# Operand and linear-attention steps of blocks 1 to 3 go two to a slot instead of one

## The chip, the cores and the metric

One core of a Trainium2 chip runs the whole kernel. The metric is device time in microseconds (us), from launch to end. The engines are PE (TensorE: matmuls, which accumulate in PSUM), DVE (VectorE), ACT (ScalarE), POOL (GpSimd) and SP (SyncE, which here only issues DMAs). Each engine works through its own list of instructions in order and waits on semaphores that others raise.

## The reference

One decoder layer on a sequence of 2048 rows of width 1024. The input projection feeds three token mixers in parallel, an output projection joins them, and a gated feed-forward part follows.

```python
h = rms_norm(x, norm1_gain) * (1.0 + scale1) + shift1
proj = h @ w_in
out_a = rg_lru(conv(xa), ...) * gelu(ya)                 # recurrence over the sequence
out_b = forgetting_attention(fq, fk, fv, ff, ...)        # 6 heads of 64, causal, RMS-normed q and k
out_c = gated_linear_attention(gq, gk, gv, glow, gg, ...)# 4 heads of 64, chunks of 64 rows
x = x + gate1 * (concatenate([out_a, out_b, out_c]) @ w_out)
h = rms_norm(x, norm2_gain) * (1.0 + scale2) + shift2
gt, up = split(h @ ffn_w_gate_up)                        # 2 x 2816 columns
x = x + gate2 * ((silu(gt) * up) @ ffn_w_down)
```

## The kernel before

The sequence is cut into four blocks of 512 columns (block 0 to block 3), everything transposed. A first function projects blocks 0 to 2 and runs their recurrence. The function that the change touches, `mix_and_feed_forward`, does the rest: the projection of block 3, and for each block the operands of the softmax attention, the linear attention, the softmax attention, the output projection and the feed-forward part.

**Units and slots.** Its backbone is a list `units` of 328 weight tiles: `p` (projection of block 3), `o` (output projection), `g` and `u` (gate and up), `d` (down). A unit is 8 (for some `d` units 6) triples of matmuls of 512 columns, since every float32 product is split into three (`split_products`, L77 to L79). A slot is one unit's place in this order. For each unit SP loads the tile, ACT rounds it to a high part (L1108), POOL subtracts it to get the low part (L1093), and PE multiplies into one of two PSUM banks (`ff_acc_ps`). The bank is read by ACT for `g` (a silu, L1280) or by DVE for `u` (L1575) and `d`. PE may start unit j + 2 only when unit j has been read. In ACT's and DVE's lists the reading of unit j stands behind all side work of slot j.

**Side work.** The table `side` hangs other work on slots. One entry is a "turn": a list of steps that PE does together between two triples of that unit; several turns in a slot are spread over its triples. ACT and DVE do the same steps in the same order, after reading unit j - 1. The work for block b sits in the slots of the unit run ahead of block b's output projection:

- `X`, steps 0 to 6, operands of the softmax attention: transposes of the values (L1718), squares and row sums (step 1 and 2, L1726), forget-gate sums on DVE (step 2, L1433 to L1447), norms (step 3, L1450 to L1459), and in steps 4 to 6 the spreading of the norms over q and k (L1744), two tiles in each, whose results SP writes to DRAM (L956, L959).
- `G`, steps 0 to 7 for each of two head pairs j, in the order `G_ORDER`: (0,0) (1,0) (0,1) (1,1) (0,2) (1,2) (0,3) (1,3) (0,4) (0,5) (0,6) (1,4) (0,7) (1,5) (1,6) (1,7), as (pair, step). Step 0 to 3 make the decays; step 2, called the gating step below, is a chain of five DVE operations (L1486 to L1497) with four exponentials on ACT behind it (L1209 to L1212). Step 4 transposes and multiplies, step 5 makes the outer products (L1772), from which DVE builds the running state in 16 dependent operations (L1522); step 6 needs the state (L1781, L1784); step 7 normalises (L1789 on PE, L1228 and L1230 on ACT, L1529 and L1533 on DVE).
- the heads of the softmax attention, as turns of `S` (scores for the maximum, L1665), `M` (the maximum turned, L1675, after DVE's L1395), `T` (scores, L1691), `V` (times the values, L1707) and `F`. A turn mostly holds one `T` and one `V`, often an `S`. They fill the slots from the end of the linear attention to six slots ahead of the block's output projection, however many those are.

`x_load`, `g_load`, `a_load`, `fill_at` and `q_fill` name the slots in which SP loads the inputs of these three parts and POOL presets their tiles. In block 0, whose side work has only the 24 `p` slots, `X` and `G` already stand two to a slot (`G0_SLOT`; steps 0 and 1 of `G` even four), set by code that the change leaves alone.

Of the kernel before, what the change touches and what calls it, by code (L numbers as in the profile page):

```python
# [42 lines left out]
GLA_T = GLA_HEADS * HEAD_DIM // P  # L43
# [513 lines left out]
def mix_and_feed_forward(nc, vec, mod, held, xT, w_in, w_gates, w_alpha, w_out, w_gate_up, w_down, consts, fox_rows, proj, mix, q_split, ka, kb, v_split, yT):  # L557
# [90 lines left out]
    X_STEPS, G_STEPS, X_LEAD, G_LEAD, A_LEAD, END = 7, 8, 3, 3, 2, 6  # L648
# [7 lines left out]
    side = {}  # L656
# [12 lines left out]
    for b in range(1, NBLK):  # L669
        turns = turns_of(b)  # L670
        lo = at["o", 0, 0, 0] + 1 if b == 1 else at["o", b - 1, KD - 1, 0] + 1
        x_load.append(lo)
        lo += X_LEAD
        for s in range(X_STEPS):
            side[lo + s] = [[("X", (b, s))]]
        lo += X_STEPS + 1
        g_load.append(lo)
        lo += G_LEAD - 1
        for x, (j, s) in enumerate(G_ORDER):
            side[lo + x] = [[("G", (b, j, s))]]  # L680
        lo += GLA_T * G_STEPS + 1
        a_load.append(lo)
        fill_at.append(lo)
        q_fill.append(lo)
        lo += A_LEAD - 1
        hi = at["o", b, 0, 0] - END
        for x, turn in enumerate(turns):
            side.setdefault(lo + x * (hi - lo) // len(turns), []).append(turn)
# [1258 lines left out]
```

## Time and profile before

| | |
|---|---|
| median of 3 runs | 2987.01 us (2985.84 to 2988.37) |
| the profiled execution's own time | 2993.32 us |
| its span, first to last instruction | 2991.5 us |
| PE busy | 2818.5 us, 94% |
| DVE, ACT, POOL busy | 49%, 40%, 35% |
| mean granted clock of TensorE | 0.973 of 2.4 GHz |
| chain that ended last | PE 64%, of it L77 to L79 49%; DVE 7%, ACT 4% |

The profiled execution took 6.3 us more than the median, so a difference read in the trace is to be set against 2993.32 us and then carried over to the median. A matmul's end in the trace is modelled, so PE counts as busy while it only drains; the time of PE is better counted by how many matmuls start in a stretch. "Granted clock" 1.00 is 2.4 GHz and 0.5 is 1.2 GHz, and a value between them is a mean over time at either.

### The profile page before, as it was taken

The page shows a single profiled execution, that of the slowest core. Times are in us where ns is not written, and L with a number is a line of the kernel's source. Part 1 is how long each engine was busy: PE and PEld are TensorE (multiplying, and loading weights), DVE is VectorE, ACT ScalarE, POOL GpSimd, SP SyncE. Part 2 cuts the span into 40 slices and gives each one's busy share as a digit, 9 for nine tenths or more (in the row PEclk, how much of TensorE's full clock was granted, in tenths as well). Part 3 has the DMA queues.
Part 4 walks back from the last instruction along what each step waited for, and adds up shares of the span by engine and source line. Part 5 has one row for each costly group of instructions (what it writes and reads, how often), then busy time and mean ns, then how long its engine had stood idle before and what let it go on. Part 6 is the DMA issues. An engine that isn't in the chain of part 4 may idle for free.

```text
span 2991.5 us, 32965 instructions
## 1 busy us (share of the span) xinstructions
PE 2818.5 (94%) x12416; PEld 2211.5 (74%) x12416; DVE 1463.1 (49%) x1876; ACT 1185.2 (40%) x1654; POOL 1035.5 (35%) x488
## 2 busy tenths in 40 slices
PE   8998998788988999999999999999999999999999
PEld 4786876466757777886777777867777777778887
DVE  3968786466564334435443454463435554421111
ACT  3333333343345244444433545454335455332222
POOL 2545453221324332243333222334332112444443
PEclk9999999789999999999999999999999999999999
DMA  7555535525644344444624454545245553423233
GB/s 266 180 167 178 166 130 162 171 78 159 220 123 138 105 134 130 130 152 145 184 74 126 140 150 123 161 149 173 74 130 150 151 150 114 144 98 96 94 99 92
DMA packets 159902, 419.05 MB, mean 140 GB/s; under 512 B 18284, under 2 KB 20604, under 8 KB 156672
## 3 DMA queue, kind: packets, MB, share of 16 engines
q1 hardware_dynamic: 157408, 412.48, 44.6%
q10 hardware_dynamic: 2336, 4.46, 0.4%
q8 instruction: 99, 1.62, 0.2%
q14 instruction: 59, 0.48, 0.1%
HBM read 355.95 MB, written 60.92 MB: 139 GB/s over the span
## 4 chain that ended last, share of the span: by engine, by line
PE 64%; DVE 7%; ACT 4%; issue 3%; DMA 3%; SPq 2%; POOL 1%; ACTq 0%; POOLq 0%; DVEq 0%
PE ff_acc_ps L77 17%; PE ff_acc_ps L78 16%; PE ff_acc_ps L79 16%; DMA ff_w_raw<-in_w_gate_up 2%; PE fa_st_ps L1691 1%; PE fa_o_ps L1707 1%; PE fa_s_ps L1665 1%; PE fa_st_ps L1692 1%; PE fa_o_ps L1709 1%; PE fa_o_ps L1708 1%; PE fa_s_ps L1666 1%; DVE ff_silu L1371 1%; DVE fa_inv_sum L1408 1%; SPq L956 1%; PE fa_o_ps L1781 1%
## 5 line engine op out<-in xcount | busy, mean ns | idle before, releaser
L1093 POOL TENSOR_TENSOR w_lo<-ff_w_raw,w_hi 128x1024 fp32r<-128x1024 f32 (+1 forms) x326 | 771.9, 2368 | 1626.7 <-PE ff_acc_ps L79 1553.7
L77 PE MATMUL ff_acc_ps<-h_odd_hi,w_hi 128*128 128x512 f32 x1856 | 752.2, 405 | 50.7 <-DVE h_odd_lo L1376 13.4
L78 PE MATMUL ff_acc_ps<-h_odd_lo,w_hi 128*128 128x512 f32 x1856 | 738.3, 398 | 0.0
L79 PE MATMUL ff_acc_ps<-h_odd_hi,w_lo 128*128 128x512 f32 x1856 | 736.7, 397 | 0.0
L1108 ACT ACTIVATE w_hi<-ff_w_raw 128x1024 fp32r<-128x1024 f32 (+1 forms) x326 | 338.7, 1039 | 935.8 <-PE ff_acc_ps L79 721.5
L77 PEld LDWEIGHTS ff_acc_ps<-h_odd_hi,w_hi 128*128 128x128 f32 x1856 | 357.2, 192 | 160.2 <-issue 63.6
L79 PEld LDWEIGHTS ff_acc_ps<-h_odd_hi,w_lo 128*128 128x128 f32 x1856 | 356.7, 192 | 78.4
L78 PEld LDWEIGHTS ff_acc_ps<-h_odd_lo,w_hi 128*128 128x128 f32 x1856 | 358.2, 193 | 72.7 <-issue 1.7
L77 PE MATMUL ff_acc_ps<-ff_a_hi,w_hi 128*128 128x512 f32 x704 | 285.2, 405 | 10.1 <-issue 6.1
L1401 DVE TENSOR_TENSOR fa_p_lo<-fa_probs,fa_p_hi 128x512 fp32r<-128x512 f32 x240 | 154.4, 644 | 286.7 <-ACT fa_p_hi L1142 286.4
L78 PE MATMUL ff_acc_ps<-ff_a_lo,w_hi 128*128 128x512 f32 x704 | 280.2, 398 | 0.0
L79 PE MATMUL ff_acc_ps<-ff_a_hi,w_lo 128*128 128x512 f32 x704 | 279.9, 398 | 0.0
L211 POOL TENSOR_TENSOR w_lo<-w_raw,w_hi 128x1024 fp32r<-128x1024 f32 x74 | 183.1, 2475 | 219.4 <-PE g_ps L79 163.2
L1141 ACT ACTIVATE fa_probs<-fa_st_ps 128x512 f32<-128x512 f32 x240 | 128.3, 535 | 230.3 <-PE fa_st_ps L1692 151.7
L1383 DVE TENSOR_REDUCE fa_ch_max<-fa_s_ps 128x1 f32<-128x512 f32 (+1 forms) x240 | 144.6, 607 | 137.9 <-PE fa_s_ps L1666 80.5
L1575 DVE TENSOR_TENSOR ff_gated<-ff_silu,ff_acc_ps 128x512 f32<-128x512 f32 x88 | 60.4, 687 | 309.0 <-PE ff_acc_ps L79 272.2
L250 ACT ACTIVATE w_hi<-w_raw 128x1024 fp32r<-128x1024 f32 x74 | 78.4, 1059 | 281.2 <-DMA w_raw<-in_w_in 254.2
L1577 DVE TENSOR_TENSOR ff_a_lo<-ff_gated,ff_a_hi 128x512 fp32r<-128x512 f32 x88 | 110.2, 1252 | 121.3 <-ACT ff_a_hi L1287 121.3
L77 PEld LDWEIGHTS ff_acc_ps<-ff_a_hi,w_hi 128*128 128x128 f32 x704 | 133.1, 189 | 46.4 <-issue 14.8
L77 PE MATMUL g_ps<-h_even_hi,w_hi 128*128 128x512 f32 x384 | 158.0, 411 | 9.8 <-POOL w_lo L211 5.6
L79 PEld LDWEIGHTS ff_acc_ps<-ff_a_hi,w_lo 128*128 128x128 f32 x704 | 133.4, 189 | 32.3
L78 PEld LDWEIGHTS ff_acc_ps<-ff_a_lo,w_hi 128*128 128x128 f32 x704 | 133.3, 189 | 32.0 <-issue 1.7
(263 smaller groups left out, 4047.5 us busy)
## 6 DMA issues: line engine op xcount, KB each, us to landing
ff_w_raw<-in_w_gate_up SPq DMA_DIRECT2D x176, 512.0 KB, 4.1
w_raw<-in_w_in SPq DMA_DIRECT2D x74, 512.0 KB, 4.3
ff_w_raw<-in_w_down SPq DMA_DIRECT2D x64, 512.0 KB, 3.6
mod_w<-in_w_mod SPq DMA_DIRECT2D x24, 1024.0 KB, 5.5
fa_v<-v_split_dram SPq DMA_DIRECT2D x60, 384.0 KB
ff_w_raw<-in_w_out SPq DMA_DIRECT2D x32, 512.0 KB, 3.9
fa_ks_a<-ka_dram SPq DMA_DIRECT2D x60, 256.0 KB
fa_kt_a<-ka_dram SPq DMA_DIRECT2D x60, 256.0 KB
```

Source lines behind the costliest of these rows:

```text
L77: nc.tensor.matmul(out, hi, act_hi, start=first, stop=False)
L78: nc.tensor.matmul(out, hi, act_lo, start=False, stop=False)
L79: return nc.tensor.matmul(out, lo, act_hi, start=False, stop=last)
L211: nc.gpsimd.tensor_tensor(w_lo[:, j % LO], w_raw[:, j % RAW], w_hi[:, j % HI].bitcast(F32), ALU.subtract).then_inc(lo_ready, 1)
L250: nc.scalar.activation(w_hi[:, j % HI], w_raw[:, j % RAW], ACT.Copy).then_inc(hi_ready, 1)
L1093: nc.gpsimd.tensor_tensor(w_lo[:, j % LO, wide], w_raw[:, j % RAW, wide], w_hi[:, j % HI, wide].bitcast(F32), ALU.subtract).then_inc(lo_re ...
L1108: nc.scalar.activation(w_hi[:, j % HI, wide], w_raw[:, j % RAW, wide], ACT.Copy).then_inc(hi_ready, 1)
L1141: nc.scalar.activation(probs[:, m % PB, r * P:], st_ps[:, m % 2, r * P:], ACT.Exp)
L1383: nc.vector.tensor_reduce(ch_max[:, U % 2, i, c:c + 1], s_ps[:, bank_of(("S", n)), 0:w], AX.X, ALU.max).then_inc(max_done, 1)
L1401: nc.vector.tensor_tensor(p_lo[:, m % PB, r * P:], probs[:, m % PB, r * P:], p_hi[:, m % PB, r * P:].bitcast(F32), ALU.subtract).then_inc( ...
L1575: nc.vector.tensor_tensor(gated[:, i % 2], silu[:, i % 2], acc, ALU.mult).then_inc(gated_ready, 1)
L1577: nc.vector.tensor_tensor(a_lo[:, i % AR], gated[:, i % 2], a_hi[:, i % AR].bitcast(F32), ALU.subtract).then_inc(a_ready, 1)
```

## The change

```diff
         x_load.append(lo)
         lo += X_LEAD
         for s in range(X_STEPS):
-            side[lo + s] = [[("X", (b, s))]]
-        lo += X_STEPS + 1
+            side.setdefault(lo + s // 2, []).append([("X", (b, s))])
+        lo += (X_STEPS + 1) // 2 + 1
         g_load.append(lo)
         lo += G_LEAD - 1
         for x, (j, s) in enumerate(G_ORDER):
-            side[lo + x] = [[("G", (b, j, s))]]
-        lo += GLA_T * G_STEPS + 1
+            side.setdefault(lo + x // 2, []).append([("G", (b, j, s))])
+        lo += GLA_T * G_STEPS // 2 + 1
         a_load.append(lo)
         fill_at.append(lo)
         q_fill.append(lo)
```

For blocks 1 to 3 the seven `X` steps take four slots instead of seven and the sixteen `G` steps eight instead of sixteen, as two turns of one step each. `X_STEPS`, `G_STEPS`, `GLA_T` are 7, 8 and 2. No computation is added or dropped. The slots come out as follows (slot numbers count from 0; the heads' columns are first and last slot).

| block | X before / after | G before / after | a_load before / after | heads before | heads after |
|---|---|---|---|---|---|
| 1 | 28-34 / 28-31 | 38-53 / 35-42 | 55 / 44 | 56-89, 34 slots, 59 turns | 45-89, 45 slots |
| 2 | 107-113 / 107-110 | 117-132 / 114-121 | 134 / 123 | 135-165, 31 slots, 87 turns | 124-165, 42 slots |
| 3 | 183-189 / 183-186 | 193-208 / 190-197 | 210 / 199 | 211-241, 31 slots, 115 turns | 200-241, 42 slots |

The first place is ACT's list at the two gating steps of block 2. Before, the four exponentials of pair 0 (the first row is the last of them) and of pair 1 stand apart, with the rounding of a weight tile (L1108) and a conversion for a `u` unit (L1287) between them:

```order
L1212 ACTIVATE ga_decay<-ga_b_cum 128x8
L1108 ACTIVATE w_hi<-ff_w_raw 128x1024
L1287 ACTIVATE ff_a_hi<-ff_gated 128x512
L1209 ACTIVATE ga_z<-ga_one_e 128x512
L1210 ACTIVATE ga_grow<-ga_b_cum 128x512
L1211 ACTIVATE ga_e_neg<-ga_b_cum 128x512
L1212 ACTIVATE ga_decay<-ga_b_cum 128x8
L1108 ACTIVATE w_hi<-ff_w_raw 128x1024
L1280 ACT_TABLE_LOAD
L1280 ACTIVATE ff_silu<-ff_acc_ps 128x512
```

Afterwards the same place of ACT reads:

```order
L1209 ACT_TABLE_LOAD
L1209 ACTIVATE ga_z<-ga_one_e 128x512
L1210 ACTIVATE ga_grow<-ga_b_cum 128x512
L1211 ACTIVATE ga_e_neg<-ga_b_cum 128x512
L1212 ACTIVATE ga_decay<-ga_b_cum 128x8
L1209 ACTIVATE ga_z<-ga_one_e 128x512
L1210 ACTIVATE ga_grow<-ga_b_cum 128x512
L1211 ACTIVATE ga_e_neg<-ga_b_cum 128x512
L1212 ACTIVATE ga_decay<-ga_b_cum 128x8
L1108 ACTIVATE w_hi<-ff_w_raw 128x1024
L1280 ACT_TABLE_LOAD
L1280 ACTIVATE ff_silu<-ff_acc_ps 128x512
```

Both pairs' exponentials now stand together, and the silu of the unit in that slot behind both of them.

The second place is DVE's list at the end of the linear attention of block 2. Before, pair 0's normalisation (L1529, L1533) has one reading of a `d` unit (L1608) between it and the 16 state operations of pair 1 (L1522):

```order
L1608 SCALAR_TENSOR_TENSOR ff_x<-ff_acc_ps,mod,ff_x 128x512
L1529 SCALAR_TENSOR_TENSOR ga_gq<-fa_o_ps,vec,ga_b_cum 128x512
L1533 TENSOR_TENSOR ga_gg<-ga_gq,ga_gg 128x512
L1608 SCALAR_TENSOR_TENSOR ff_x<-ff_acc_ps,mod,ff_x 128x512
L1522 SCALAR_TENSOR_TENSOR ga_state<-ga_state,ga_decay,fa_st_ps 64x64 x16
```

Afterwards:

```order
L1577 TENSOR_TENSOR ff_a_lo<-ff_gated,ff_a_hi 128x512
L1529 SCALAR_TENSOR_TENSOR ga_gq<-fa_o_ps,vec,ga_b_cum 128x512
L1533 TENSOR_TENSOR ga_gg<-ga_gq,ga_gg 128x512
L1522 SCALAR_TENSOR_TENSOR ga_state<-ga_state,ga_decay,fa_st_ps 64x64 x16
L1526 COPY ga_carry<-ga_state 128x128
```

The normalisation is now in the same slot as pair 1's step 5, directly ahead of the state operations, and the units around it are `g` and `u` units instead of `d` units. In PE's list the distances shrink with it: the number of projection matmuls between the row sums of `X` step 2 and the first spreading matmul (L1744) falls from 48 to 24, and between the outer products (L1772) and the step that needs the state (L1781) from 24 to 15.

## Rows read from the trace of the kernel before

**Rows 1.** The page: span, then busy time, share and instructions of each engine.

```profile
span 2991.5 us, 32965 instructions
...
PE 2818.5 (94%) x12416; PEld 2211.5 (74%) x12416; DVE 1463.1 (49%) x1876; ACT 1185.2 (40%) x1654; POOL 1035.5 (35%) x488
...
PEclk9999999789999999999999999999999999999999
```

**Rows 2.** Windows, projection matmuls alone: start:end, length, busy (count), clock, DMA share.

```profile
2641.50:2711.00 69.50, 69.50 (x308) 1.00 0.30 93
2185.10:2533.80 348.70, 198.40 (x769) 0.99 0.48 139
615.30:671.70 56.40, 28.24 (x97) 0.85 0.27 85
2112.00:2174.20 62.20, 47.56 (x194) 1.00 0.20 64
```

**Rows 3.** Waits of PE, 1038 to 2534 us: total, times, longest.

```profile
PE fa_s_ps L1675 <- DVE fa_m_cols L1395: 12.6, 11, 2.2
PE ff_acc_ps L77 <- ACT ff_silu L1280: 8.4, 3, 4.0
...
PE fa_s_ps L1665 <- DMA fa_ks_b<-kb_dram: 5.9, 3, 2.9
...
PE fa_s_ps L1665 <- DVE fa_ch_max L1383: 4.5, 8, 0.9
```

**Rows 4.** Timeline of DVE, block 0, two gating steps in one slot: start, duration.

```profile
605.03 2.45 DVE L1486 SCALAR_TENSOR_TENSOR ga_one_e<-ga_one_e,ga_e_neg 128x512 f32<-128x512 f32 x1
...
611.19 2.72 DVE L1497 TENSOR_TENSOR ga_one_e<-ga_b_cum 128x512 f32<-128x512 f32 x1
...
617.25 0.69 DVE L1497 TENSOR_TENSOR ga_one_e<-ga_b_cum 128x512 f32<-128x512 f32 x1
```

**Rows 5.** Timeline of ACT, same place.

```profile
619.56 0.20 ACT L1212 ACTIVATE ga_decay<-ga_b_cum 128x8 f32<-128x8 f32 x1
```

**Rows 6.** Timeline of ACT, block 2, the second gating step and what follows.

```profile
1511.27 1.04 ACT L1108 ACTIVATE w_hi<-ff_w_raw 128x1024 fp32r<-128x1024 f32 x1
1512.32 1.28 ACT L1280 ACT_TABLE_LOAD   x1
1513.62 0.60 ACT L1280 ACTIVATE ff_silu<-ff_acc_ps 128x512 f32<-128x512 f32 x1
```

**Rows 7.** Timeline of PE right behind it.

```profile
1514.32 0.47 PE L77 MATMUL ff_acc_ps<-ff_a_hi,w_hi 128*128 128x512 f32 x1 [3.07 <-issue]
```

**Rows 8.** Windows, all engines: PE, PEld, DVE, ACT, POOL busy (count), clock.

```profile
1511.00:1521.70 10.70, 7.63 (x27) 5.90 (x26) 3.54 (x6) 5.69 (x9) 2.35 (x1) 0.84 0.24 81
```

**Rows 9.** Timeline of DVE, block 2: state chain of head pair 0, normalisation of its output.

```profile
1534.00 4.96 DVE L1522 SCALAR_TENSOR_TENSOR ga_state<-ga_state,ga_decay,fa_st_ps 64x64 f32<-64x64 f32 x16 [3.16 <-PE fa_st_ps L1772]
...
1561.11 0.75 DVE L1529 SCALAR_TENSOR_TENSOR ga_gq<-fa_o_ps,vec,ga_b_cum 128x512 f32<-128x512 f32 x1 [5.59 <-ACT ga_b_cum L1230]
1561.89 2.41 DVE L1533 TENSOR_TENSOR ga_gg<-ga_gq,ga_gg 128x512 f32<-128x512 f32 x1
```

**Rows 10.** Timeline of PE, block 0, output step of pair 1.

```profile
658.08 0.87 PE L1781 MATMUL fa_o_ps<-ga_e_neg,ga_state 128*128 128x64 f32 x4 [4.24 <-issue]
```

**Rows 11.** Timeline of DVE, block 2, operand steps 2 and 3.

```profile
1412.25 0.68 DVE L1433 SCALAR_TENSOR_TENSOR fp_rows<-fp_rows 6x512 f32<-6x512 f32 x1 [1.76 <-ACT fp_rows L1176]
...
1416.55 0.68 DVE L1447 TENSOR_TENSOR fp_bias_lo<-fp_rows,fp_bias_hi 6x512 fp32r<-6x512 f32 x1
...
1423.02 0.67 DVE L1450 TENSOR_SCALAR fp_rows<-fa_s_ps 12x512 f32<-12x512 f32 x1
...
1429.72 0.68 DVE L1459 TENSOR_TENSOR fp_rows<-fp_rows 12x512 f32<-12x512 f32 x1
```

**Rows 12.** Timeline of PE, row sums of step 2 and spreading of step 4, block 2.

```profile
1413.90 2.74 PE L1726 MATMUL fa_s_ps<-fp_squares,fp_rows_sel 128*12 128x512 f32 x6
...
1430.46 1.98 PE L1744 MATMUL fa_st_ps<-fp_rows,fp_back_sel 12*128 12x512 f32 x4 [2.31 <-DVE fp_rows L1459]
```

## The prediction

> **What bounds the kernel now.** I read the page first: PE is busy 94% of the span, DVE 49% and ACT 40% [rows 1]. So only time that PE spends waiting, or at the lower clock, can be won or lost; side work itself costs PE the same wherever it stands. Then I counted projection matmuls in windows. At the end, where block 3's feed-forward part runs with no side work, 308 of them start in 69.50 us, 0.226 us each, so a bare unit of 24 takes 5.42 us [rows 2]. That is the yardstick: a stretch's length less 0.226 us per projection matmul is what side work and waiting cost there. In the head slots of block 3 this is 348.7 - 769 x 0.226 = 175 us [rows 2]. Third, the waits of PE over blocks 1 to 3: in the head part it waited 12.6 us for the turned maximum, 5.9 us for a key load, 4.5 us for a bank that DVE had not yet reduced [rows 3]. The 8.4 us for a late silu are three waits, two of them (the longest 4.0 us) at the start of a head part. So of 175 us in block 3 nearly all is matmuls of the heads, and the heads' dependences cost PE only about 23 us in all three blocks.
>
> **What more slots can give the heads.** 261 turns now stand in 96 slots and will stand in 129, so the distance between turns grows by a third. The three waits above, 12.6 + 5.9 + 4.5 = 23.0 us, are the upper bound; nothing is the lower. The wait for the maximum is DVE's chain behind the last reduction, at most 2.2 us at a time, and about one more unit share between turns (a slot of 4 turns becomes one of 3: 5.42/3 - 5.42/4 = 0.45 us) takes away part of it. I take 10 us.
>
> **What two steps to a slot cost.** A bare slot is 5.42 us. Steps that were one slot apart are now half a slot or a whole slot's share apart, so every chain through DVE and ACT has half the cover. Block 0 already runs this way and shows the prices.
>
> Gating steps. Two of them are ten DVE operations, from 605.03 to 617.25 + 0.69 = 617.94 us in block 0: 12.9 us [rows 4]. ACT's last copy ends at 619.56 + 0.20 = 619.76 us [rows 5], 14.7 us after the start. Behind it stand, in a `g` slot (blocks 2 and 3), the rounding, a table load and the silu, 1.04 + 1.28 + 0.60 = 2.92 us [rows 6]. PE may start the unit after next only after that silu. It gets there two bare units, 10.8 us, after the slot's start, and DVE starts about when the slot does. So PE waits 14.7 + 2.9 - 10.8 = 6.8 us, up to 9 where DVE first has a conversion of a `u` unit. This wait exists now at the second gating step, with one step to a slot, at 3.07 us [rows 7], and it took the clock to a mean of 0.84 over 10.7 us, another 1.7 us [rows 8]. I take 8 us of wait and 3 us of clock less the 4.8 us of now: +6 us in each of blocks 2 and 3. In block 1 the slot is a `u` slot: DVE's own reading (L1575) stands behind the 12.9 us, a wait of 12.9 - 10.8 + 0.7 = 2.8 us, and then step 4 waits for three products more: 7 us in all with the clock, less the 4.8 us of now: about +4.
>
> State chain. 16 dependent operations take 4.96 us [rows 9]; PE has 24 matmuls, 5.4 us, between outer products and step 6 now, and will have 15, 3.4 us: +1.6 us at pair 0. At pair 1 the 16 operations stand behind pair 0's normalisation, 0.75 + 2.41 us [rows 9], which waits for ACT. Block 0 has this order, and PE waited 4.24 us there [rows 10]. I take 5 us, since DVE's L1533 is the slow form here: together +6.6 us a block.
>
> Clock. The last four `G` slots of block 0 hold 97 projection matmuls in 56.4 us, so 56.4 - 21.9 = 34.5 us of side cost, at a mean clock of 0.85; the same steps one to a slot in block 3 cost 62.2 - 43.8 = 18.4 us at 1.00 [rows 2]. The difference is 16 us, of which 0.15 x 56.4 = 8.5 us is clock. Block 0 has recurrence work on DVE and ACT beside it, so I take 3 us of clock for these slots. For `G` in all: 15.6 us in blocks 2 and 3, 13.6 in block 1, together 45 us. Bounds: a third of it, 15, if the chains start earlier than I place them, and 3 x 16 + 12 = 60.
>
> Operand steps. In block 2 DVE works on step 2 from 1412.25 to 1416.55 + 0.68 = 1417.23 us, and on step 3, with ACT between, from 1423.02 to 1430.40 us: 5.0 + 7.4 = 12.4 us of chain [rows 11]. PE waited 2.31 us for its end, with 48 matmuls, 10.8 us, between the row sums and the first spreading [rows 12]. With 24 matmuls it has 5.4 us less: about +6 us, with 1.5 us of clock, in blocks 2 and 3. In block 1 the following slot already stands still for the norm of the feed-forward part, so PE only waits earlier: +2 us. Together 17; bounds 5 and 25.
>
> Loads. In block 1 the burst of head loads moves from `d` slots to `g` and `u` slots. In blocks 2 and 3 it stands at `g` and `u` slots already and there a silu came up to 4.0 us late [rows 3]; afterwards it stands at the last `u` slot ahead of `d` slots. +3 us for block 1, nothing for the others; between 0 and 8.
>
> No queue gets more to do on SP and POOL: the same DMAs, but step 4 and 5 issue 18 stores in one slot. ACT's order has 159 table loads instead of 146, as more `g` slots lie between exponentials: 13 x 1.28 us [rows 6] on an engine at 40%, so nothing on PE's path; if ACT were the bound it would be 17 us.
>
> **Sum.** 45 + 17 + 3 - 10 = +55 us. Against the profiled execution, 2993.3 + 55 = 3048; the median lies 6.3 us lower, so 2987 + 55 = 3042 us, 1.8% slower. By the bounds: 15 + 5 + 0 - 23 = -3 us and 60 + 25 + 8 - 0 = +93 us, all at one end at once.
>
> **A rule against the change.** The row shows the clock at a mean of 0.84 right behind a 3.07 us wait [rows 7, 8], so half speed follows a wait of that size. By that, each new wait of 3 us or more costs some 1.7 us more, and that is in my clock terms. The Trainium skill (TensorE: Matmul & The Clock Gate, section Why this matters for your kernels) advises against idle gaps between bursts of matmuls, because the array falls back to half its clock; by that rule alone the change, which makes gaps, is wrong whatever else it does. The trace agrees in direction.
>
> **Rivals.**
> 1. *The clock stays low.* Waits of 7 to 9 us, two or three within 60 us, keep PE at 1.2 GHz between them as in block 0, where the mean was 0.85 over 56.4 us [rows 2]. Then X and G of each block lose 8.5 us more: 2987 + 55 + 25 = 3067, up to 3090. Against: in block 0 gates and recurrence crowd the same slots. Chance 0.15.
> 2. *The chains are mostly hidden.* DVE has no recurrence work in blocks 1 to 3, and if it starts each chain while PE is still in the slot before, only the state chain and half of the others remain: +15 to +30 us less 10: about 3000. Against: steps are tied to a slot on every engine, and the wait exists now at one step to a slot [rows 7]. Chance 0.12.
> 3. *The other side: faster.* The heads are limited by the distance between turns, and each saves waiting. It decides if new waits stay below the heads' gain; at most 23 us can be gained [rows 3], and the waits of rows 7 and 12 would not have to grow. 2987 - 12 = 2975. Chance 0.05.
> 4. *No effect*, because waits of X and G take the place of others that go (the late silu, the norm ahead of the first `g` unit). Against: the sizes, 45 us to cancel. Chance 0.03, 2987.
>
> **How the numbers follow.** My forecast, 3042, has 0.65; its own range is 3018 to 3062. The range 3005 to 3070 leaves out most of rivals 3 and 4, part of 2 and of 1, near 0.2. Within 0.2% (6 us, about what a measurement can tell from no change) I put 0.03; slower by more 0.92; faster by more 0.05.
>
> **What would show it.** After the change: at L1280 behind two pairs of L1209 to L1212, a wait of PE of 6 to 9 us in blocks 2 and 3; L1781 idle 1.6 us at pair 0 and about 5 us at pair 1, three times; L1744 waiting for L1459 7 to 9 us in blocks 2 and 3; more stretches at 1.2 GHz around these slots; L1675's 12.6 us down to some 5. X and G stretches of each block longer by 15 to 22 us than now less the dropped slots' bare units, head stretches shorter than 33 x 5.42 us more than now. I am wrong if the yardstick (length less 0.226 us per projection matmul) over X and G does not grow, or if it falls by more than 23 us over the heads: then turns cost each other something that the waits don't show.

## The result, and the profile after

Over four runs each, the changed kernel took 3059.39 us in the median (3054.22 to 3062.57), the kernel before 2986.43 us (2979.22 to 2988.37). The ratio is 1.0252 with a 95% interval of 1.0236 to 1.0268: 2.5% slower, 73 us. The profiled execution took 3060.68 us, so the trace may stand for the median as it is. The page of the changed kernel:

```profile
span 3058.9 us, 32978 instructions
...
PE 2848.1 (93%) x12416; PEld 2229.2 (73%) x12416; DVE 1450.4 (47%) x1876; ACT 1203.8 (39%) x1667; POOL 1037.3 (34%) x488
...
PEclk9999999789988999998989999998899999999999
```

Against [rows 1], the instruction counts of PE and DVE are the same, and ACT has 13 more, the table loads. PE counts as busy 30 us longer for the same matmuls, and six further slices have the clock digit 8 instead of 9. The span grew by 67 us.

Where it went is read as the prediction proposed, from windows of the projection matmuls (start:end, length, busy with count, clock, DMA share). First block 2 before, in three stretches: `X` with the gap behind it, `G`, and the rest up to the block's first `o` unit.

```profile
1390.50:1470.60 80.10, 59.20 (x236) 0.96 0.60 184
1470.60:1583.90 113.30, 93.62 (x386) 0.98 0.25 82
1583.90:1923.10 339.20, 227.36 (x914) 0.99 0.48 141
```

Block 2 after, the same three, and `G` of block 3:

```profile
1403.40:1480.90 77.50, 44.31 (x162) 0.82 0.56 166
1480.90:1564.90 84.00, 50.90 (x194) 0.90 0.19 63
1564.90:1962.90 398.00, 287.83 (x1178) 0.99 0.45 134
2091.20:2183.00 91.80, 55.23 (x193) 0.83 0.19 63
```

Length less 0.226 us a matmul is the side cost, by the prediction's yardstick. `G` of block 2 goes from 113.3 - 386 x 0.2257 = 26.2 us to 84.0 - 194 x 0.2257 = 40.2 us. The same for all stretches, in us, blocks 1 / 2 / 3:

| | X and gap | G | heads |
|---|---|---|---|
| before | 40.3 / 26.8 / 27.8 | 26.7 / 26.2 / 26.2 | 84.2 / 132.9 / 175.8 |
| after | 38.2 / 40.9 / 34.7 | 39.7 / 40.2 / 48.2 | 90.2 / 132.1 / 174.9 |
| sum of the difference | +18.9 | +49.0 | +4.3 |

The sum, 72.2 us, is what the kernel lost, to a few us: the spans differ by 67 us, and the changed kernel reaches the first of these stretches 4 us earlier. The yardstick is a little short for `d` units: in the kernel before, 46 matmuls of bare `d` units start from 1027.27 to 1038.04 us, 0.234 us apart. The 24 `d` slots that the heads gained and `G` lost make 24 x 24 x 0.008 = 4.8 us of it, so the heads lost and won about nothing. The waits of PE from block 1's heads to block 3's last, which answer to [rows 3]:

```profile
PE ff_acc_ps L77 <- ACT ff_silu L1280: 21.7, 5, 7.2
PE fa_st_ps L1744 <- DVE fp_rows L1459: 16.8, 2, 8.6
PE fa_s_ps L1665 <- DVE fa_ch_max L1383: 15.6, 3, 7.0
PE fa_o_ps L1781 <- issue: 9.1, 4, 3.1
PE fa_s_ps L1675 <- DVE fa_m_cols L1395: 8.9, 5, 2.3
...
PE fa_s_ps L1665 <- DMA fa_ks_b<-kb_dram: 2.9, 3, 2.1
```

The late silu, the spreading and the state step were foreseen. The third row was not: `L1665` waited 0.9 us at most for a bank before, now 7.0 us.

The chains, each in block 2. ACT behind the two gating steps, and PE behind ACT, which answer to [rows 5 to 7]:

```profile
1510.72 0.20 ACT L1212 ACTIVATE ga_decay<-ga_b_cum 128x8 f32<-128x8 f32 x1
...
1511.88 1.28 ACT L1280 ACT_TABLE_LOAD   x1
1513.17 0.60 ACT L1280 ACTIVATE ff_silu<-ff_acc_ps 128x512 f32<-128x512 f32 x1
```

```profile
1513.92 0.76 PE L77 MATMUL ff_acc_ps<-h_odd_hi,w_hi 128*128 128x512 f32 x1 [7.15 <-ACT ff_silu L1280]
```

The silu of that slot ends 3 us behind the last exponential, and PE stood still for 7.15 us for it. Next the state chain on DVE and PE, which answers to [rows 9, 10]:

```profile
1545.68 0.69 DVE L1533 TENSOR_TENSOR ga_gg<-ga_gq,ga_gg 128x512 f32<-128x512 f32 x1
1546.29 4.96 DVE L1522 SCALAR_TENSOR_TENSOR ga_state<-ga_state,ga_decay,fa_st_ps 64x64 f32<-64x64 f32 x16
```

```profile
1528.31 0.63 PE L1781 MATMUL fa_o_ps<-ga_e_neg,ga_state 128*128 128x64 f32 x4 [1.48 <-issue]
...
1551.35 0.66 PE L1781 MATMUL fa_o_ps<-ga_e_neg,ga_state 128*128 128x64 f32 x4 [3.06 <-issue]
```

The outer products of pair 1 were done at 1544.6 us, but DVE had the normalisation of pair 0 in front, so the 16 operations began at 1546.29 us and PE waited 3.06 us. Last the operand steps on PE, which answer to [rows 12]:

```profile
1412.56 4.08 PE L1726 MATMUL fa_s_ps<-fp_squares,fp_rows_sel 128*12 128x512 f32 x6 [3.96 <-ACT fp_squares L1152]
...
1436.94 3.78 PE L1744 MATMUL fa_st_ps<-fp_rows,fp_back_sel 12*128 12x512 f32 x4 [8.58 <-DVE fp_rows L1459]
```

### The profile page after: what moved, and what is told of

Same layout as the page of the kernel before. It is cut to its first block, busy times and chain, and to the rows that moved or that the text cites. A ratio compares the mean times of both kernels' runs of the same rounds, so it can differ in the third digit from the quotient of the medians.

```text
span 3058.9 us, 32978 instructions
## 1 busy us (share of the span) xinstructions
PE 2848.1 (93%) x12416; PEld 2229.2 (73%) x12416; DVE 1450.4 (47%) x1876; ACT 1203.8 (39%) x1667; POOL 1037.3 (34%) x488
## 4 chain that ended last, share of the span: by engine, by line
PE 65%; DVE 7%; ACT 3%; issue 3%; DMA 3%; SPq 2%; POOL 1%; ACTq 0%; DVEq 0%; POOLq 0%
PE ff_acc_ps L77 17%; PE ff_acc_ps L78 16%; PE ff_acc_ps L79 16%; PE fa_o_ps L1707 2%; PE fa_st_ps L1691 2%; PE fa_s_ps L1665 2%; PE fa_st_ps L1692 2%; PE fa_s_ps L1666 1%; PE fa_o_ps L1709 1%; PE fa_o_ps L1708 1%; DMA ff_w_raw<-in_w_gate_up 1%; PE fa_st_ps L1744 1%; PE fa_o_ps L1781 1%; DVE fa_inv_sum L1408 1%; DVE ff_silu L1371 1%
## 5 line engine op out<-in xcount | busy, mean ns | idle before, releaser
L1108 ACT ACTIVATE w_hi<-ff_w_raw 128x1024 fp32r<-128x1024 f32 (+1 forms) x326 | 338.8, 1039 | 939.1 <-PE ff_acc_ps L79 782.1
L77 PEld LDWEIGHTS ff_acc_ps<-h_odd_hi,w_hi 128*128 128x128 f32 x1856 | 359.4, 194 | 169.2 <-issue 80.1
L1575 DVE TENSOR_TENSOR ff_gated<-ff_silu,ff_acc_ps 128x512 f32<-128x512 f32 x88 | 60.4, 686 | 295.6 <-PE ff_acc_ps L79 262.7
L1577 DVE TENSOR_TENSOR ff_a_lo<-ff_gated,ff_a_hi 128x512 fp32r<-128x512 f32 x88 | 113.6, 1291 | 120.7 <-ACT ff_a_hi L1287 120.7
L77 PEld LDWEIGHTS ff_acc_ps<-ff_a_hi,w_hi 128*128 128x128 f32 x704 | 133.3, 189 | 40.1 <-issue 9.3
```

What stands on the lines that cost most here:

```text
L77: nc.tensor.matmul(out, hi, act_hi, start=first, stop=False)
L1108: nc.scalar.activation(w_hi[:, j % HI, wide], w_raw[:, j % RAW, wide], ACT.Copy).then_inc(hi_ready, 1)
L1577: nc.vector.tensor_tensor(a_lo[:, i % AR], gated[:, i % 2], a_hi[:, i % AR].bitcast(F32), ALU.subtract).then_inc(a_ready, 1)
```

## The experiments

The edits stand against the changed kernel unless the text says otherwise. Side costs are worked out from windows as above, in us; to be read against the table above. "Eleven empty slots" is the changed kernel with the heads started late.

| kernel | X and gap | G | heads |
|---|---|---|---|
| only X paired | 42.0 / 35.1 / 34.5 | 26.3 / 30.9 / 30.9 | 80.1 / 121.6 / 180.8 |
| only G paired | 36.6 / 26.7 / 27.5 | 41.3 / 43.8 / 41.4 | 90.4 / 126.0 / 161.8 |
| eleven empty slots | 38.2 / 39.5 / 40.5 | 39.9 / 38.9 / 39.0 | 83.6 / 131.9 / 176.5 |
| heads dense | 36.5 / 25.2 / 26.1 | 30.8 / 26.4 / 26.3 | 86.5 / 135.5 / 189.0 |
| gating steps alone | 37.9 / 37.9 / 40.5 | 37.8 / 39.3 / 39.5 | 90.8 / 124.6 / 168.2 |
| three empty slots | 37.2 / 39.4 / 34.4 | 38.4 / 40.6 / 47.7 | 89.3 / 125.8 / 162.5 |
| state step first | 38.6 / 40.6 / 34.8 | 31.9 / 32.7 / 36.9 | 90.9 / 132.3 / 176.8 |
| gap in X | 38.3 / 36.8 / 36.6 | 39.1 / 40.2 / 40.3 | 90.3 / 124.4 / 170.7 |
| X4 alone | 38.5 / 40.1 / 38.5 | 40.5 / 38.6 / 40.5 | 91.1 / 132.3 / 175.7 |
| free pairs of G | 38.7 / 25.2 / 25.8 | 31.7 / 23.7 / 25.1 | 79.7 / 120.9 / 177.2 |
| free pairs of both | 39.3 / 36.3 / 35.0 | 29.1 / 20.6 / 20.8 | 88.4 / 122.1 / 168.8 |
| the same, G kept | 32.1 / 34.7 / 33.5 | 24.8 / 21.1 / 21.1 | 80.3 / 121.7 / 176.3 |

How far these can be read shows in the kernels whose `X` and `G` are those of the changed one (eleven and three empty slots). In blocks 1 and 2 they agree within 1.7 us; in block 3 `X` lies between 34.4 and 40.5 us and `G` between 39.0 and 48.2. In the changed kernel a silu comes 3.06 us late at 2094.20 us, as `G` of block 3 begins, and the clock is 0.50 from 2095 to 2105 us. With eleven empty slots that wait is 1.07 us, and the clock falls before it, in `X` (0.71 between 2080 and 2085 us). So a gain of up to 9 us in `G` of block 3 alone may have nothing to do with an edit.

### Each half of the change by itself

Only the `X` hunk of the diff, and only the `G` hunk, on the kernel before.

> The kernel before with only the operand steps X of blocks 1 to 3 two to a slot; the heads get three slots more. Theory A (the loss is chains through DVE and ACT that lost their cover, each paired slot at its own price): the trace of the changed kernel puts 27 us on X and -8 us on the stretch between X and G, so +17 to +22 us, L1744 waiting about 8 us in blocks 2 and 3. Theory B (the loss comes with the earlier start of the heads: their load burst and their exponentials among silus, 11 slots of it): 3 of 11 slots, +5 us or less. What I predicted for this part was +17.

> The kernel before with only the linear attention steps G of blocks 1 to 3 two to a slot; the heads get eight slots more. Theory A: +45 to +55 us, with silu waits of 7 us in blocks 2 and 3, L1781 idle about 1.5 and 3 us in every block, and the sum of this and of X alone is the whole change, +73 us. Theory B: 8 of 11 slots of it, about the same +50 us, but then the linear attention stretches would hold little of it and the head stretches most. What I predicted for this part was +45.

`X` paired took 2999.10 us (ratio 1.0053, 1.0037 to 1.0069), `G` paired 3019.27 us (1.0121, 1.0103 to 1.0138), beside 2984.41 us. That is 15 and 36 us, 51 together, where the whole change costs 73. The stretches of `X` and `G` grew as they do in the whole change (`X` +16.7, `G` +47.4), but the heads' stretches shrank: by 15.4 us over blocks 1 and 2 with `X` paired (block 3's grew by 5.0), by 20.9 us over blocks 2 and 3 with `G` paired (block 1's grew by 6.2). `G` grew by 9.1 us where only `X` was paired. `X` and `G` together do add up, 25.8 and 43.3 us against 67.9 in the whole change; the heads do not. So something in the heads depends on where they begin, not on how many slots they have.

### Heads with few slots

The changed kernel with the heads started where they started before; and the kernel before with its heads squeezed into eleven slots fewer.

```diff
-        lo += GLA_T * G_STEPS // 2 + 1
+        lo += GLA_T * G_STEPS // 2 + 1 + 11
```

```diff
-    X_STEPS, G_STEPS, X_LEAD, G_LEAD, A_LEAD, END = 7, 8, 3, 3, 2, 6
+    X_STEPS, G_STEPS, X_LEAD, G_LEAD, A_LEAD, END = 7, 8, 3, 3, 2, 17
```

> The changed kernel, X and G two to a slot, but with 11 empty slots behind G, so that the heads start in the same slots as in the kernel before. Theory A: the pairs still cost all they cost, +65 to +78 us over before, no better and no worse than the changed kernel by more than 8 us. Theory B: the loss goes with the heads' start, so it falls to +20 us or less. My prediction's term for the heads (11 more slots save 10 us) would make this kernel 10 us slower than the changed one.

> The kernel before with END 17 instead of 6: the heads of each block end 11 slots earlier, so 87 turns stand in 20 slots instead of 31 in block 2 and 115 in 20 in block 3. If the distance between turns matters for PE (my term of -10 us for 11 slots more), 11 slots fewer cost 10 to 30 us. If turns cost the same at any distance, as the head stretches of both traces suggest (the side cost there differs by 1.2 us in blocks 2 and 3), it is within 5 us of before.

The first took 3050.31 us (ratio 1.0231, 1.0210 to 1.0251): without the eleven slots the kernel was not slower than with them but 9 us faster by the medians; the two intervals overlap, so the 9 us are not shown. The second took 3007.72 us (1.0090, 1.0069 to 1.0111); its heads cost 2.3, 2.6 and 13.2 us more in blocks 1, 2 and 3. Density clearly costs something only in block 3, at nearly six turns to a slot. In the range in which the change moves it no gain from more slots is seen.

### Three more empty slots: the place of the head loads

In the changed kernel `a_load` is slot 123 in block 2 and 199 in block 3, the last `u` slot ahead of a run of `d` slots. Three empty slots behind `G` put the burst three slots into that run.

```diff
-        lo += GLA_T * G_STEPS // 2 + 1
+        lo += GLA_T * G_STEPS // 2 + 1 + 3
```

> The changed kernel with three empty slots behind G: the load burst of the heads and their first steps fall on the third slot of the d units in blocks 2 and 3, as they did where only G was in pairs, instead of the last u slot ahead of them. Theory C (X alone and G alone cost 15 and 36 us, 51 together, and both together 73, because the place of the heads' load burst changes): the 7.0 us wait at L1665 goes in blocks 2 and 3, the X and G stretches stay, and it is 15 to 25 us faster than the changed kernel, with 3 slots fewer for the heads. If the pairs of X and G disturb each other instead, it stays within 5 us of the changed kernel.

It took 3038.43 us (ratio 1.0178, 1.0163 to 1.0193), 21 us under the changed kernel, with `X` and `G` of each block within 1.5 us and the heads down by 6.3 us in block 2 and 12.4 us in block 3. The trace shows the mechanism. In the changed kernel, ACT's and DVE's rows behind the burst of block 2:

```profile
1585.99 1.06 ACT L1108 ACTIVATE w_hi<-ff_w_raw 128x1024 fp32r<-128x1024 f32 x1 [10.08 <-DMA ff_w_raw<-in_w_down]
1586.96 0.61 ACT L1287 ACTIVATE ff_a_hi<-ff_gated 128x512 fp32r<-128x512 f32 x1
```

```profile
1587.60 0.69 DVE L1577 TENSOR_TENSOR ff_a_lo<-ff_gated,ff_a_hi 128x512 fp32r<-128x512 f32 x1 [10.91 <-ACT ff_a_hi L1287]
```

```profile
1588.95 0.80 PE L1665 MATMUL fa_s_ps<-fa_ks_a,fa_q_a 128*128 128x512 f32 x1 [6.99 <-DVE fa_ch_max L1383]
```

Read from the bottom up: PE waits 6.99 us for DVE to empty a bank, DVE waits 10.91 us for ACT's conversion of the last `u` unit, and ACT has a weight rounding in front of that conversion, for which it waits 10.08 us, because the tile, issued by SP behind 14 loads of the heads, has not landed. With the burst in the middle of `d` slots ACT waits longer still for its tile, and the windows (all engines, here 1590 to 1600) show PE busy without a break:

```profile
1599.94 1.06 ACT L1108 ACTIVATE w_hi<-ff_w_raw 128x1024 fp32r<-128x1024 f32 x1 [13.65 <-DMA ff_w_raw<-in_w_down]
```

```profile
1590.00:1600.00 10.00, 10.00 (x45) 8.10 (x44) 3.94 (x6) 0.06 (x1) 2.41 (x1) 1.00 1.01 313
```

`d` units are read by DVE alone, so nothing that PE needs soon is queued behind ACT's waiting rounding; `u` and `g` units are read through ACT. In block 2 this holds over the whole table: the heads cost 120.9 to 126.0 us in the eight kernels whose burst falls in a `d` slot, and 131.9 to 135.5 us in the six others.

In blocks 1 and 3 it is not the whole. With `X` paired, and with the free pairs below, the burst of block 3 falls in a `d` slot too (207), and the heads cost 176.3 to 180.8 us, no less than before. There `L1675`, the turned maximum, waited 9.0 us. Its wait in block 3 follows neither the burst nor the number of slots: 4.3 us with 31 slots, 9.0 with 34, none listed with 36, 0.2 to 0.3 with 39, 5.6 with 41, 3.6 with 42. Of the 12.4 us that three empty slots gained in block 3, 6.8 are less waiting at `L1665` and 3.3 less at `L1675`. How the turns fall on the slots is what is left as a cause; no run separates it.

### The gating steps in slots of their own

```diff
-        for x, (j, s) in enumerate(G_ORDER):
-            side.setdefault(lo + x // 2, []).append([("G", (b, j, s))])
-        lo += GLA_T * G_STEPS // 2 + 1
+        for at_slot, (j, s) in zip((0, 0, 1, 1, 2, 3, 4, 4, 5, 5, 6, 6, 7, 7, 8, 8), G_ORDER):
+            side.setdefault(lo + at_slot, []).append([("G", (b, j, s))])
+        lo += 9 + 1
```

> The changed kernel, but the two gating steps of each block stand in slots of their own (nine slots for G instead of eight, so heads start one slot later). If a pair of gating steps is what makes the silu late, its wait falls from 7.2 to about 3 us in blocks 2 and 3 and the 5.2 us wait of step 4 in block 1 goes: 12 to 18 us less than the changed kernel with the clock, all of it on the G stretches. If the price is the crowding of the slots in general, the G stretches keep their 40 to 48 us and the kernel stays within 5 us, apart from what the later start of the heads does.

It took 3036.13 us (ratio 1.0164, 1.0147 to 1.0181), 23 us less, more than expected. But 14 us of that lies in the heads of blocks 2 and 3, whose burst moved to the first `d` slot. In `G` of block 2 the waits of PE were

```profile
PE ff_acc_ps L77 <- ACT ff_silu L1280: 4.6, 2, 3.1
PE fa_o_ps L1781 <- issue: 4.5, 2, 3.0
```

so the longest wait fell from 7.2 us to 3.1, and yet the stretch cost 39.3 us instead of 40.2. Some of the 4 us went to a lower clock: the clock's part (length times one less the mean clock; an upper bound, since a wait at half clock loses nothing) of block 2's `G` is 10.6 us here and 8.4 in the changed kernel. The rest I can't place. In block 3 `G` fell by 8.7 us, but to the 39.5 us that it costs with eleven empty slots (39.0) with its gating steps still paired, and `X` grew by 5.8 us as it does there. So the gating pair is worth 1.9 and 0.9 us in blocks 1 and 2, and in block 3 no gain is shown: not the full wait anywhere.

### The state step ahead of the other pair's normalisation

The last four steps in the order (1,5) (0,7) (1,6) (1,7) instead of (0,7) (1,5) (1,6) (1,7), in the same slots.

```diff
-        for x, (j, s) in enumerate(G_ORDER):
+        for x, (j, s) in enumerate(G_ORDER[:12] + [(1, 5), (0, 7), (1, 6), (1, 7)]):
```

> The changed kernel with steps (0,7) and (1,5) exchanged in blocks 1 to 3, so that pair 1's 16 state operations stand ahead of pair 0's normalisation on DVE. If that order is what PE waits for, the second idle time at L1781, 3.1 us in each block, falls below 1 us, and with the clock the kernel is 8 to 15 us faster than the changed one. If it is only the length of the state chain, 5 us against 3.5 us of matmuls, the idle time stays near 1.6 us or above and little is won, under 5 us.

It took 3039.03 us (3031.88 to 3051.11; ratio 1.0183, 1.0156 to 1.0210), 20 us less, more than the 8 to 15 expected. The profiled execution was the fastest, 7 us under the median, so the trace shows 29 us of difference. `G` fell by 7.8, 7.5 and 11.3 us, `X` and the heads stayed within 2 us a block. The waits of PE in `G` of block 2, and its window:

```profile
PE ff_acc_ps L77 <- ACT ff_silu L1280: 8.9, 2, 7.1
PE fa_o_ps L1781 <- issue: 1.5, 1, 1.5
```

```profile
1470.10:1546.60 76.50, 48.97 (x194) 0.96 0.20 69
```

Only the wait of 3.06 us is gone, and the clock's part fell from 8.4 to 76.5 x 0.04 = 3.1 us: 3.06 + 5.3 is a little over the 7.5 us. One wait of 3 us cost 7.5.

### A gap ahead of the spreading, and X4 by itself

An empty slot between `X` steps 3 and 4 (everything later moves by one); and step 5 moved from step 4's slot to step 6's.

```diff
-            side.setdefault(lo + s // 2, []).append([("X", (b, s))])
-        lo += (X_STEPS + 1) // 2 + 1
+            side.setdefault(lo + s // 2 + s // 4, []).append([("X", (b, s))])
+        lo += (X_STEPS + 1) // 2 + 2
```

```diff
-            side.setdefault(lo + s // 2, []).append([("X", (b, s))])
+            side.setdefault(lo + (0, 0, 1, 1, 2, 3, 3)[s], []).append([("X", (b, s))])
```

> The changed kernel with one empty slot between X steps 3 and 4 of blocks 1 to 3 (G and the heads one slot later). If the missing slots between row sums and spreading are the price of X, the wait at L1744 falls from 8.6 and 8.2 us to about 3 us in blocks 2 and 3 and from 3.9 us to nothing in block 1, and the X stretches get 12 to 20 us shorter with the clock. If the price lies in the squares that now stand ahead of the norm of the feed-forward part (4.0 and 3.9 us at L1726), the X stretches shorten by less than 6 us.

> The changed kernel with one step moved: X5 stands with X6 and not with X4; the operand steps still take four slots, and nothing else moves. Theory (X4 and X5 in one slot are the dear pair: 25.7 us in block 2 against 19.1 us in two slots before): L1744 still waits 8 us in blocks 2 and 3, but X's stretches lose 4 to 9 us a block, with clock time in them, 3035 to 3050 us. Rival (only the wait of L1744 matters, and X5's work costs the same in any slot): X's stretches stay within 2 us a block, 3055 to 3063 us.

The gap took 3034.19 us (ratio 1.0161, 1.0146 to 1.0176), 25 us less, but mostly elsewhere than its theory said: 12 us lie in the heads and 8 us in block 3's `G` (which is down to what eleven empty slots gave it), and `X` with its gap gained 4.1 us in block 2 and lost 1.9 us in block 3. The waits of PE in `X` of block 2 were

```profile
PE ff_acc_ps L77 <- ACT ff_silu L1280: 4.6, 1, 4.6
PE fa_s_ps L1726 <- ACT fp_squares L1152: 4.0, 1, 4.0
```

The 8.6 us at `L1744` are gone and a silu is 4.6 us late in their place. Step 5 moved changed nothing: 3058.15 us (1.0248, 1.0228 to 1.0269). There `L1744` waited 6.9 us instead of 8.6, and three slots later PE stood still for a weight tile. The wait, and the window around it for all engines:

```profile
PE ff_acc_ps L77 <- POOL w_lo L1093: 6.1, 1, 6.1
```

```profile
1471.30:1486.00 14.70, 8.71 (x26) 6.88 (x27) 2.05 (x2) 3.12 (x4) 7.78 (x6) 0.65 0.94 317
```

That is where SP issues the loads of `G`: the DMA engines are 94% busy at 317 GB/s. In the changed kernel they were as busy there (95%, 1471.3 to 1481 us) and this wait was 2.5 us. So `L1744` waited 1.7 us less and the weight tile 3.6 us more: what PE gained in front of the loads, it lost again at them.

### Pairs only where they are free

From the pairs that I took to be free by the runs above: the kernel before with `G` steps 0 and 0, 1 and 1, and 3 of pair 1 with 4 of pair 0 in one slot, all others alone, and both gating steps in `u` slots with (0,3) between them. `G` takes 13 slots instead of 16. So three things change at once: the pairs, the unit under the gating steps, and the place of the burst, in `d` slots in all three blocks.

```diff
-        for x, (j, s) in enumerate(G_ORDER):
-            side[lo + x] = [[("G", (b, j, s))]]
-        lo += GLA_T * G_STEPS + 1
+        for at_slot, (j, s) in zip((0, 0, 1, 1, 2, 3, 4, 5, 5, 6, 7, 8, 9, 10, 11, 12), G_ORDER[:5] + [(0, 3), (1, 2), (1, 3)] + G_ORDER[8:]):
+            side.setdefault(lo + at_slot, []).append([("G", (b, j, s))])
+        lo += 13 + 1
```

> The kernel before with its single steps, but for those pairs that the runs so far showed at no cost: G's two first steps of both tiles (0 with 0, 1 with 1), and step 3 of the second tile with step 4 of the first. The two gating steps stand alone, both in u slots (step 3 of the first tile between them). G takes 13 slots, not 16, so the burst of head loads falls in d slots 7 of blocks 2 and 3, where it stood in g slots 9. Theory (pairs cost by what they hold, and the burst by its place): G's stretch loses the silu wait of 3.1 us with 1.7 us of clock in blocks 2 and 3 (24.8 to about 20 us of side cost), the burst costs 5 to 10 us less in blocks 2 and 3, the heads gain 2 to 3 us a block from three slots more: 2955 to 2975 us, 10 to 30 under the kernel before. Rival (any pair costs, and the place of the burst is chance): 2985 to 3005 us.

It took 2966.99 us (2958.65 to 2969.71), a ratio of 0.9939 (0.9923 to 0.9954) to the kernel before: 18 us or 0.6% faster, within the 10 to 30 expected, but not in the parts expected. `G` of blocks 2 and 3 cost 3.6 us less together, not some 10 (block 1's 5.0 more), `X` 5.2 us less and the heads 15.1 us less in all: 12.0 in block 2, 4.4 in block 1, and 1.4 more in block 3, where 7 to 13 less were expected. The kernel with only `X` paired, whose bursts fall in the same slots, shows the same heads (4.1 and 11.3 less, 5.0 more). So the three pairs were about free, and the gain came from where the heads begin, not from the pairs; the kernel before with only its burst moved was not run. In `G` of block 2 PE waited twice:

```profile
PE fa_st_ps L1772 <- ACT ga_v_n L1221: 1.3, 1, 1.3
PE fa_o_ps L1781 <- issue: 1.0, 1, 1.0
```

The late silu of 3.07 us that the kernel before had here is gone, since a `u` unit does not wait for one.

Then with `X` in the slots X0 X1 / X2 X3 / empty / X4 / X5 X6, once with everything behind it two slots earlier than in the version above, once with `G` and the heads kept in its places.

```diff
-            side[lo + s] = [[("X", (b, s))]]
-        lo += X_STEPS + 1
+            side.setdefault(lo + (0, 0, 1, 1, 3, 4, 4)[s], []).append([("X", (b, s))])
+        lo += 5 + 1
```

> f2_free_pairs with the operand steps too in those pairs that cost nothing in the runs so far: X0 with X1, X2 with X3, an empty slot, X4 alone, X5 with X6; five slots, not seven. The burst moves to d slots 5 of blocks 2 and 3, the heads get two slots more. Theory: X costs the same as before within 2 us a block (X0 with X1 took 14.9 us in one slot, where the two took 19.3 in two), the heads gain 1 to 2 us a block: 2950 to 2970 us, up to 8 under f2_free_pairs. Rival: L1744 waits again, since it now stands two slots nearer to the normalisation ahead of it: 5 us a block in blocks 2 and 3, and the time is 5 to 12 us over f2_free_pairs.

> f3_free_pairs_both with two empty slots between the operand steps and the loads of G, so that G, its loads, the head loads and the heads stand where f2_free_pairs has them; only the operand steps are paired (X0 with X1, X2 with X3, a gap, X4, X5 with X6). In f3_free_pairs_both a wait of 5.2 us for w_lo stood two slots ahead of G in blocks 2 and 3, with the DMA queues full, since G's loads meet the block's own loads there. Theory (the pairs cost little, and f3 lost its time to where G's loads fell): the wait for w_lo goes back to 2 to 3 us, X's stretches stay 4 to 5 us over those of f2_free_pairs in blocks 2 and 3: 2970 to 2978 us. Rival (the pairs themselves cost what f3 lost): 2978 to 2985 us. In no case is it faster than f2_free_pairs by more than 2 us, since the heads get no slot more.

The first took 2980.98 us (ratio 0.9991, 0.9979 to 1.0002), the second, with `lo += X_STEPS + 1`, 2969.88 us (0.9940, 0.9925 to 0.9955), no different from the version above: its `X` cost 10.6 us more and its `G` 13.5 us less. So the place of everything behind `X` decides 15 us (by the ratios), and the pairs of `X` nothing in sum. Not where it was expected, though. The waits of PE over `X` of block 2, first of the earlier placing, then of the kept one:

```profile
PE ff_acc_ps L77 <- POOL w_lo L1093: 5.2, 1, 5.2
PE ff_acc_ps L77 <- ACT ff_silu L1280: 4.4, 1, 4.4
```

```profile
PE ff_acc_ps L77 <- ACT ff_silu L1280: 8.9, 2, 4.4
```

The wait for the weight tile only turned into one for a silu of 4.4 us at the same loads, and block 2 differs by 1.5 us. The 15 us lie in block 1, 19.6 us over its three stretches, less 6.3 in block 3. In block 1's heads `L1675` waited 7.5 us in the earlier placing and 2.1 us in the kept one, which goes with the 8.1 us there; why `X` and `G` of block 1 are better too was not tried.

## Why the prediction was right, and where it was not

Predicted were 3042 us, range 3005 to 3070; measured were 3059. The direction and the place (`X` and `G`, not the heads) were right, the sum was 17 us short: 2 us of it in `X`, 4 to 9 in `G`, 7 to 11 in the heads with their loads. Term by term:

- **Gating steps.** Right in size of the wait: 6.8 us by the chain, 8 taken, 7.15 us in block 2 and 7.1 in block 3. In block 1, 2.8 us were forecast at the unit's bank and more at step 4; measured were 0.9 and 5.2 us. But alone in their slots the two steps gave back only 1.9 us in block 1 and 0.9 in block 2, against the +4 and +6 forecast, and in block 3 nothing that can be put to them. The long wait is real, but in block 2 the clock's part of `G` did not fall when it was cut to 3.1 us (10.6 us against 8.4).
- **State chain.** At pair 0 forecast 1.6, measured 1.48 us. At pair 1 forecast 5, measured 3.06 us: `L1533` was not in its slow form (0.69 us, not the 2.41 of [rows 9]). The cause, the normalisation in front, is shown by the exchange of the two steps. The two waits are 4.5 us a block where 6.6 were forecast; that they cost more in the end is the clock, below.
- **Clock.** This is the term that was mis-sized. I put 3 us a block for `G` beside what the gating term held. The clock's part of `G`, an upper bound, rose from 2.3 to 10.0, 8.4 and 15.6 us in blocks 1, 2 and 3, that is by 7.7, 6.1 and 13.3 us. I had counted half speed once for a big wait, at the size of [rows 8]. It also follows the 3.06 us wait at `L1781`, as the exchange showed, and costs 5.2 us there and not the 1.7 of [rows 8]. `G` in all: forecast 45, measured 49, or 54 with the dropped `d` units reckoned at their own pace. That it comes so near is partly luck: smaller waits and more clock nearly cancelled.
- **Operand steps.** Forecast +17, measured +18.9 with the gap. `L1744` waited 8.58 us in block 2, within the 7 to 9. Not forecast: `L1726` waits 4.0 us instead of 1.7, and removing `L1744`'s wait by a gap removes only 4 us in block 2, because a silu is late next. The size was right, but the mechanism was told too simply: several chains end within a few us of each other.
- **Heads.** Forecast -10. The step that failed was that one more unit share between turns takes away part of the wait for the maximum, and nothing else grows. `L1675` did fall from 12.6 to 8.9 us and the key load from 5.9 to 2.9, but `L1665` rose from 4.5 to 15.6 us, and with the loads the heads' stretches came out at +4.3 us, or about 0 with the `d` units at their own pace. Nor does `L1675` wait less the more slots there are: 9.0 us in block 3 with 34 slots, 4.3 with 31, so that its fall was partly luck.
- **Loads.** Forecast +3, for block 1 alone, "nothing for the others". Heads and loads together were forecast at -7 and came out 7 to 11 us above that. That the burst costs no more in blocks 2 and 3 than where it stood held in the total (132.9 and 132.1 us, 175.8 and 174.9), but only because it was dear in both places: three slots later the heads cost 6.3 and 12.4 us less, and `L1665` waits 6.0 and 6.8 us less. I had read its cost before as one late silu, and did not ask which engine waits for the weight tile behind the burst and what is queued behind that engine. In the two halves of the change the burst and the heads fall elsewhere, and so they add up to 51 us and not to 73.

Of the rivals, the first (the clock stays low, 3067 to 3090) was partly true: clock accounts for at most 27 us of `G`'s growth and 14 of `X`'s, but between the waits it came back to 1.00. The Trainium skill (TensorE: Matmul & The Clock Gate, section Why this matters for your kernels) advises against idle gaps between bursts of matmuls, since the array then falls back to half its clock. This case's trace agrees: behind the wait of 3.06 us the clock fell to 0.50, and the wait cost 7.5 us in all. The second, third and fourth rivals are ruled out by the time. The third was wrong in its cause as well: with the heads delayed by eleven slots nothing was lost, and where heads did get cheaper it went with the place of the burst and the waits of `L1675`.

## What to carry to other kernels

A slot table should pair only steps that put no longer chain through another engine in front of PE: here three of the eight pairs of `G` cost about nothing (1.3 us over three blocks), while the pairs of `X` and `G` together made the kernel 2.5% slower. The version with the free pairs was 0.6% faster than before, but for where its heads begin. Where a burst of loads delays the stream of weights, look for the engine that waits for the late tile and for what stands behind it in that engine's list; put the burst where that list holds nothing that the matmuls need. When the start of a stage moves, its cost moves with where its loads fall, so the parts of a change measured alone need not add up (15 + 36 us against 73). Read such a kernel stage by stage, and against a second kernel with the same stage, before a gain is put to an edit.

## What was not expected of the hardware

The price of half speed did not grow with the wait. Windows of PE in block 2 of the changed kernel, 5 us each, the first with the shorter wait in it, the third with the longer:

```profile
1525.00:1530.00 5.00, 3.52 (x25) 1.00 0.17 53
1530.00:1535.00 5.00, 5.00 (x36) 1.00 0.15 55
...
1545.00:1550.00 5.00, 3.29 (x15) 1.00 0.51 149
1550.00:1555.00 5.00, 3.65 (x20) 0.68 0.03 11
1555.00:1560.00 5.00, 5.00 (x20) 0.50 0.00 0
1560.00:1565.00 5.00, 5.00 (x17) 0.79 0.00 0
```

The first wait, 1.48 us, left the clock at 1.00. The second, of 3.06 us, ended at 1551.35 us; the mean from there to 1565 gives (0.32 + 0.50 + 0.21) x 5 = 5.2 us lost, so some 10 us at 0.50 (1.2 GHz), all of it on work. In windows of 1 us, the end of this wait, and the middle of the wait of 7.15 us for the silu, which lasted from 1506.8 to 1513.9 us:

```profile
1551.00:1552.00 1.00, 0.65 (x6) 0.91 0.00 0
```

```profile
1510.00:1511.00 1.00, 0.00 (x0) 0.93 0.00 0
1511.00:1512.00 1.00, 0.00 (x0) 0.50 0.00 0
...
1517.00:1518.00 1.00, 1.00 (x8) 0.66 0.12 45
```

The short wait was over when the clock fell; the long one still had 3 us to go, and that part of the slow stretch cost nothing. Its slow stretch ended at about 1517.7 us, so 3.8 us of it lay on work, 1.9 us lost. So the wait of 3.06 us cost more than twice its length, with 5.2 us of clock behind it, and the longer one cost less clock than that; I had reckoned some 1.7 us for each wait of 3 us or more. The other wait of 3.06 us, at 2094.20 us in block 3, was dear too: the means 0.95, 0.50, 0.50 and 0.68 of the four windows of 5 us from 2090 us make 6.8 us lost.

The same DVE operation took 0.69 us or 2.72 us (`L1497` of the two pairs, 6 us apart). POOL was in a tensor operation from 1501.47 to 1504.51 us, over most of the slow one:

```profile
1502.35 2.72 DVE L1497 TENSOR_TENSOR ga_one_e<-ga_b_cum 128x512 f32<-128x512 f32 x1
...
1508.42 0.69 DVE L1497 TENSOR_TENSOR ga_one_e<-ga_b_cum 128x512 f32<-128x512 f32 x1
```

No run separated the two engines, but the two traces hold many more cases. `L1577`, which reads two tiles in SBUF, ran 88 times in the trace of the kernel before. It took 0.69 us in the 16 executions that met no tensor operation of POOL. The other 72, 0.71 to 2.47 us long, all began while one of POOL's was under way, and 71 of them ended 0.54 to 0.56 us behind its end; here 1502.35 + 2.72 = 1505.07 us, 0.56 us behind POOL's 1504.51. Where DVE was first, POOL paid: all six scans (`L1495`) of the kernel before took 1.23 us, and the POOL operation that began within each took 2.62 to 3.38 us instead of 2.4. `L1575`, which reads one tile in SBUF and one in PSUM, took 0.67 to 0.69 us in all 88 executions, 75 of them over a POOL operation that kept its 2.4 us as a rule. So the traces show one of the two waiting for the other's end, for DVE operations with both inputs in SBUF. This is also what I had called the slow form of `L1533` in [rows 9]: POOL was at work from 1561.35 to 1563.76 us there, and in the changed kernel `L1533` of pair 0 fell between two POOL operations.
